# A decoder step's conv state leaves the chip in 44 narrow transposes instead of 5 wide ones

## The chip, the cores and the metric

The kernel runs on one core of a Trainium2 chip. The metric is the time of the device for one execution, in microseconds (us); lower is better. A core has TensorE (PE), VectorE (DVE), ScalarE (ACT), GpSimd (POOL) and SyncE (SP, which only issues transfers here). Each takes its instructions in order.

## The reference, cut to what matters

One inference step of a two-layer decoder (an S5 layer, then an attention layer called FoX), for a prompt of 512 tokens and 8 decode samples of one token. Each layer ends in a feed-forward block with a causal convolution of width 3:

```python
def causal_dwconv(u, prev, w, b):
    ext = jnp.concatenate([prev.astype(u.dtype), u], axis=1)
    y = ext[:, 0:t] * w[0] + ext[:, 1:1 + t] * w[1] + ext[:, 2:2 + t] * w[2]   # written as a loop
    return y + b, ext[:, t:]              # the last two rows are the new state

def conv_ffn(h, w_up, cw, cb, w_down, prev):
    u = h @ w_up                          # 1024 -> 5632
    y, new_prev = causal_dwconv(u, prev, cw, cb)
    g, val = jnp.split(y, 2, axis=-1)
    return (jax.nn.silu(g) * val) @ w_down, new_prev      # 2816 -> 1024
```

The state that is returned has two rows of 5632 floats for the prompt, and two for each of the 8 samples. The older sample row is a copy of an input. So ten rows of `u` come from the chip in each layer: the last two of the prompt and one of each sample.

## The kernel before, in words

Activations lie with the model dimension on the 128 partitions and the 520 tokens (512 + 8) along the free axis. A product goes panel by panel: a panel is 128 output columns of a weight matrix. SP loads its raw weights into one of two buffers (`weights`, L654), ACT rounds them to a high part (`w_hi`, L2311), POOL subtracts to get a low part (`w_lo`, L1001), and PE multiplies high by high, high by low and low by high for each block of 128 inputs, in two halves of the tokens (264 and 256 columns; `product`, L2872). Two slots of weights and two pairs of PSUM banks (`big`) alternate, so that PE works on one panel while the next is prepared.

The feed-forward block of layer `l` runs `up{l}0` (22 panels), `down{l}0` (8 panels over the first half of the 2816 inputs), `up{l}1` (22) and `down{l}1` (8, over the second half). In the up phases DVE scales a panel into `uc`, ACT copies the ten columns of the state into `newconv` (L2722) and makes the first tap of the convolution, and DVE makes the rest. There are 44 column tiles of 128 in all, one after each up panel.

`down{l}1` is where the state leaves. PE multiplies panels 0 to 5 one by one, and panels 6 and 7 together (`last_pair`, L2954), because the norm behind them wants the first half of the tokens early. DVE adds each panel to `y` (L1948) and sums its squares (L1252), ACT squares it. After panel 0 PE transposes `newconv`, which is laid out as [128, 10 rows, 44 tiles], in 5 transposes of 88 columns each (two rows x 44 tiles) with the helper `turn` (L3069), into two banks of the ring `misc`. DVE copies the banks into `crows`, which is the pair `yc` under another name (L1958), and SP stores row by row: 10 transfers of 44 pieces of 512 bytes, issued after the weights of panel 4 of `down{l}1` (`conv_out`, L842).

The PSUM ring `misc` has four banks. Its jobs are numbered in one list (`misc_jobs`), PE takes a bank when the reader of the job four before has freed it, and the two sides count on the same list. The ring of `crows` buffers is freed by counting finished stores (`crows_out`). Behind `down01` SP issues a plain copy of the older sample rows from input to output (L641), and then the weights of the next phase, `win1` (L654). ACT rounds the first of these panels early, into a buffer of its own (`hi_first`, L2316), between its squares of panel 6 and of panel 7 (L2660).

Of the kernel before, what the change touches and what calls it, by code (L numbers as in the profile page):

```python
# [28 lines left out]
P = 128  # L29
# [82 lines left out]
def misc_jobs():  # L112

    jobs = [("lam",), ("rows",), ("xsT",)] + [("xT", k) for k in range(KD)] + [("ms", "x0", 0), ("ms", "x0", 1)]
    jobs += [("memT", a) for a in range(4)] + [("conv", l, a) for l in range(2) for a in range(2)]
    jobs += [("cT", 0), ("ms_mem",)] + [("state", l, a) for l in range(2) for a in range(2)]
    jobs += [("h0", ri, a) for ri in range(2) for a in range(2)]
    inputs = [[*[("bT", t, a) for a in range(TP // 2)], *[("V", t, a) for a in range((TP + 2) // 3)]]
              for t in range(THIRDS)]
    jobs += [("memtok", 0, m) for m in range(3)] + inputs[0] + [("memtok", 0, 3)] + [("memtok", 1, m) for m in range(4)]  # L120
    for t in range(THIRDS):
        jobs += inputs[t] if t else []
        jobs += [("Y", 0, a) for a in range(TG // 4) if t == 1]
        jobs += [("K", t, a) for a in range(TG // 4)] + [("qrow", 0, 1)] * (t == 0) + [("cT", t + 1)] * (t + 1 < THIRDS)
        jobs += [("Y", 1, a) for a in range(TG // 4) if t == 1]
    for a in range(0, TG // 4, 2):
        jobs += [("mq", 0, a + b) for b in range(2)] + [("Y", THIRDS - 1, a + e) for e in range(2)]
    jobs += [("mq", 0, b) for b in (4, 5)] + [("OT", 0, p) for p in LAST[0]] + [("fin", ri) for ri in range(2)]
    jobs += [("mq", 0, b) for b in (6, 7)]
    for l in range(2):  # L130
        if l == 0:
            jobs += [("mmaxT", l), ("mmax", l), ("mden", l), ("mpv", l), ("mfin", l)]
        else:
            jobs += [("qrow", l, a) for a in range(2)] + [("q", b, a) for b in range(2) for a in range(2)]
            jobs += [("qrow", l, 2)]
            for m in range(12):
                jobs += [("kvtok", m), ("kvsamp", m)]
                jobs += [("logf",)] * (m == LOGF_AT) + [("dtot",), ("dc", 0)] * (m == DECAY_AT) + [("dc", 1)] * (m == DECAY_AT + 1)
                jobs += [("q", b, a) for b in Q_PANEL if Q_PANEL[b] == m for a in range(2)]
            jobs += [("mpv", l), ("fpv", PV_BESIDE), ("mfin", l), ("fpv", PV_BESIDE + 1)]  # L140
        jobs += [("ms", f"o{l}", 0), ("ms", f"o{l}", 1), ("ms", f"f{l}", 0), ("ms", f"f{l}", 1)]
        jobs += [("cout", l, a) for a in range(2)]
        jobs += [("ms", f"d{l}", 0), ("ms", f"d{l}", 1)]
        if l == 0:
            jobs += [("ms", "x1", 0), ("ms", "x1", 1)]
    jobs += [("yT", c, a) for c, a in TURNED_OUT]
    return {name: j for j, name in enumerate(jobs)}
# [22 lines left out]
    return enumerate((n, k) for n in range(2) for k in range(KD))  # L170


CONV_ROWS = 2 * 2 * KF
CONV_SETS = ((0, 4), (4, 5))


FOX_PAIRS = HEADS // 2
# [143 lines left out]
def program(nc, I, O):  # L321
# [4 lines left out]
    with ctx:  # L326

        def sb(name, shape, dt=F32):
            return ctx.enter_context(nc.sbuf_tensor(name, shape, dt))
# [10 lines left out]
        convw = sb("convw", [P, 2, 4 * 2 * KF])  # L340
        convs = sb("convs", [P, 2, 2 * NB, 2 * KF])
        newconv_at = nc.sbuf_base
        newconv = sb("newconv", [P, 2 + NB, 2 * KF])
        stats_at = nc.sbuf_base
        rstd = sb("rstd", [P, NT])
        sd = sb("sd", [P, NT])
# [287 lines left out]
        def _(sp):  # L634
# [197 lines left out]
            weights("glu", cols(I["w_glu"][0]), beside_glu, start=2)  # L832
            weights("wout0", cols(I["w_out"][0]))

            def conv_out(l):

                for a_, (first, end) in enumerate(CONV_SETS):
                    sp.wait_ge(s_("crows_ready"), 2 * l + a_ + 1)
                    for r in range(2 * first, 2 * end):
                        dst = O["prompt_ffn_conv"][l, 0, r] if r < 2 else O["sample_ffn_conv"][l, r - 2, 1]  # L840
                        at = (r % 2) * 2 * KF
                        sp.dma_start(dst.rearrange("(t p) -> t p", p=P),  # L842
                                     crows[a_][at:at + 2 * KF, (r // 2 - first) * P:(r // 2 - first + 1) * P]
                                     ).then_inc(s_("crows_out"), 16)

            def page_id(n):
                return sp.value_load(pages[0:1, bass.ds(n, 1)], min_val=0, max_val=I["cache_k"].shape[0] - 1)
# [13 lines left out]
            def ffn_weights(l):  # L861
                if l == 0:
                    sp.wait_ge(s_("stored"), 16 * stores[0])
                    sp.wait_ge(s_("pages_in"), 16)
                for f in range(2):
                    wu = I["w_up"][l].rearrange("(k p) n -> p k n", p=P)

                    def up(i, wu=wu, f=f):

                        it, half = i  # L870
                        return wu[:, :, bass.ds(it * P + (f * KH + half * KF) * P, P)]

                    kb, n, base, _ = PH[f"up{l}{f}"]
                    with sp.Fori(0, KH) as it:
                        for half in range(2):
                            slot = (base + half) % 2
                            sp.wait_ge(lo_made, it * 2 + (base + half - 1))
                            sp.dma_start(raw[slot][:, 0:KD, :], up((it, half))).then_inc(raw_loaded[slot], 16)
                        for n in range(4 if l == f == 0 else 0):
                            past_logf(it * 4 + n)  # L880
                    weights(f"down{l}{f}", cols(I["w_down"][l], (f * KH * P, (f + 1) * KH * P)),
                            (lambda i: conv_out(l) if i == 4 else None) if f else None if l else rest_logf)

                store(O["sample_ffn_conv"][l, :, 0, :], I["state_ffn_conv"][l, :, 1, :])

# [84 lines left out]
                store(dst[:, 512 * a_:512 * a_ + 512], ytok[c][0:(P if c < 4 else NB), 512 * a_:512 * a_ + 512])  # L970

            sp.wait_ge(s_("stored"), 16 * stores[0])
            sp.wait_ge(s_("crows_out"), 16 * 2 * (2 + NB))
            for s in range(2):
                sp.wait_ge(s_(f"ktok_out{s}"), 16 * 3)


        @block.gpsimd
        def _(pool):
# [171 lines left out]
            def head_zeros(i):  # L1151

                if i in (3, 4):
                    pool.wait_ge(lo_made, PH["win1"][2] + i + 1)
                if i == 3:
                    pool.wait_ge(s_("crows_out"), 16 * (2 + NB))
                    own.tell(pool.memset(kh[DH:P, :, :], 0.0), s_("heads_set"), 1)
                    own.sync()
                elif i == 4:
                    own.tell(pool.memset(qh[DH:P, :, :], 1.0), s_("heads_set"), 2)  # L1160
                    own.sync()
                elif i == 5:
                    own.tell(pool.memset(kvs[:], 0.0), s_("heads_set"), 3)
                elif i == 6:
                    diagonal()
# [67 lines left out]
        def _(dve):  # L1233
# [707 lines left out]
            def copy_out(ph, add=None, conv=None):  # L1941

                for m in range(6):
                    q = PH[ph][2] + m
                    dve.wait_ge(panel_done, q + 1)
                    for n_, (c0, c1) in enumerate(HALF):
# [3 lines left out]
                            tell(ins, panel_read, q + 1)  # L1950
                        else:
                            do(ins)
                    for a_, (first, end) in enumerate(CONV_SETS) if conv is not None and m == 0 else ():
                        full(dve, ("cout", conv, a_))
                        if conv:
                            dve.wait_ge(s_("crows_out"), 16 * (2 + NB))
                        c = slice(0, (end - first) * P)
                        freed(own, V.tensor_copy(crows[a_][0:CONV_ROWS, c], bank(("cout", conv, a_))[0:CONV_ROWS, c]),  # L1958
                              ("cout", conv, a_))
                        mark(s_("crows_ready"))  # L1960
                    sum_step(m)
# [333 lines left out]
        def _(act):  # L2295
# [417 lines left out]
            def ffn(l):  # L2713
                for f in range(2):
# [3 lines left out]
                    def work(it, half):  # L2718
                        fb = it + (f * KH + half * KF)
                        uu, yy = uc[half], yc[half]  # L2720
                        act.wait_ge(panel_read, it * 2 + (base + half + 1))
                        A.activation(newconv[:, :, bass.ds(fb, 1)].rearrange("p t a -> p (t a)"),  # L2722
                                     uu[:, T:T + 2 + NB], ACT.Copy).then_inc(act_step, 1)

                        act.wait_ge(s_("h_made"), it + (done + 1))
# [105 lines left out]
        def _(pe):  # L2831
# [615 lines left out]
            def ffn(l):  # L3447
                for f in range(2):
# [9 lines left out]
                    for m in range(n - 2):  # L3458
                        product(base + m, (base + m) % 2, kb, h_half, HALF, h_made if m == 0 else None)
                        if m == 0:  # L3460
                            pe.wait_ge(s_("tap_made"), 44 * (l + 1))
                            rows_ = newconv[:].rearrange("p r t -> p (r t)")
                            for a_, (first, end) in enumerate(CONV_SETS):
                                o = take(("cout", l, a_))
                                for n_ in range(first, end):
                                    ins = turn(o[0:CONV_ROWS, (n_ - first) * P:(n_ - first + 1) * P],
                                               rows_[:, CONV_ROWS * n_:CONV_ROWS * (n_ + 1)], P)
                                give(ins, ("cout", l, a_))
                    last_pair(f"down{l}1", h_half, f"d{l}")

            ffn(0)
# [238 lines left out]
```

## Time and profile before

| | us |
|---|---|
| median of 3 runs | 1484.91 |
| lowest, highest | 1484.53, 1489.85 |
| the profiled execution | 1484.91 |
| its span in the profile | 1483.2 |
| PE busy | 1395.6 |
| DVE, ACT, POOL busy | 958.5, 576.4, 638.0 |

The profiled execution is itself the median, and 1.7 us of it lie outside the span of the profile. PE is the engine with the most work; how far the others matter has to be read stage by stage.

### The profile page before, as it was taken

How to read it: one execution, taken by the hardware profiler on the slowest of the kernel's cores; microseconds unless marked ns; L12 is line 12 of the kernel's file. 1: busy time of each engine (PE TensorE's matmuls, PEld its weight loads, DVE VectorE, ACT ScalarE, POOL GpSimd, SP SyncE). 2: the span in 40 equal slices, each digit the busy share in tenths (PEclk: the TensorE clock that was granted, in tenths of full speed). 3: DMA queues.
4: the chain of work that ended last, by engine and by line, in shares of the span. 5: the costliest groups of instructions: out<-in, count | busy, mean ns of one | idle time of the engine just before them, and what ended most of it. 6: DMA issues, size and time to landing. Idle time of an engine off the chain costs nothing.

```text
span 1483.2 us, 33390 instructions
## 1 busy us (share of the span) xinstructions
PE 1395.6 (94%) x12587; PEld 1299.3 (88%) x12587; DVE 958.5 (65%) x1606; ACT 576.4 (39%) x1025; POOL 638.0 (43%) x416
## 2 busy tenths in 40 slices
PE   6988878989999999999899989999999999999998
PEld 6986667989999999999889956557889999999997
DVE  5779887577772177765657788653676761377755
ACT  4554355354432134323434235432454431243323
POOL 1589432303444334442369878302214343343441
PEclk9997889999999999999999999999999999999999
DMA  6363364313333233332337669995222333233331
GB/s 174 103 146 74 66 160 137 100 46 100 88 99 100 76 86 98 93 102 87 91 86 203 198 194 308 323 338 157 84 60 85 95 97 92 80 91 93 112 90 59
DMA packets 289761, 180.53 MB, mean 122 GB/s; under 512 B 54264, under 2 KB 275468, under 8 KB 289600
## 3 DMA queue, kind: packets, MB, share of 16 engines
q1 hardware_dynamic: 289088, 179.07, 41.8%
q8 instruction: 65, 1.06, 0.3%
q14 instruction: 32, 0.26, 0.1%
q10 hardware_dynamic: 576, 0.13, 0.0%
HBM read 167.10 MB, written 10.63 MB: 120 GB/s over the span
## 4 chain that ended last, share of the span: by engine, by line
PE 66%; DVE 11%; issue 9%; POOL 6%; ACT 3%; SPq 2%; DMA 2%; DVEq 0%; ACTq 0%; POOLq 0%
PE big L2872 54%; PE big L2954 3%; SPq L638 1%; PE misc L3069 1%; DVE y L1900 1%; POOL s5s L1005 1%; POOL e_tmp L1005 1%; DVE x L1909 1%; DVE x_lo L1327 1%; POOL w_lo L1001 1%; PE misc L2939 1%; PE misc L3209 1%; POOL e_r L1005 1%; DVE sc L2096 1%; PE big L2986 1%
## 5 line engine op out<-in xcount | busy, mean ns | idle before, releaser
L1001 POOL TENSOR_TENSOR w_lo<-raw,w_hi 128x1024 fp32r<-128x1024 f32 (+2 forms) x151 | 388.9, 2576 | 696.2 <-ACT w_hi L2311 467.3
L2311 ACT ACTIVATE w_hi<-raw 128x1024 fp32r<-128x1024 f32 (+2 forms) x172 | 191.3, 1113 | 552.1 <-PE big L2872 529.9
L2872 PE MATMUL big<-x_hi,w_hi 128*128 128x264 f32 (+1 forms) x1948 | 398.3, 286 | 5.5 <-DVE x_lo L1325 1.6
L2872 PE MATMUL big<-x_hi,w_lo 128*128 128x264 f32 (+1 forms) x1948 | 392.9, 283 | 0.0
L2872 PE MATMUL big<-x_lo,w_hi 128*128 128x264 f32 (+1 forms) x1948 | 391.1, 282 | 0.0
L2872 PEld LDWEIGHTS big<-x_hi,w_hi 128*128 128x128 f32 x1948 | 299.7, 188 | 9.8 <-issue 3.2
L2872 PEld LDWEIGHTS big<-x_lo,w_hi 128*128 128x128 f32 x1948 | 299.4, 188 | 0.0
L2872 PEld LDWEIGHTS big<-x_hi,w_lo 128*128 128x128 f32 x1948 | 299.3, 188 | 0.0
L1997 DVE SCALAR_TENSOR_TENSOR yc<-uc,convw,yc 128x512 f32<-128x512 f32 x88 | 137.2, 1559 | 112.6 <-ACT yc L2726 112.6
L2872 PE MATMUL big<-h_hi,w_hi 128*128 128x264 f32 x616 | 124.4, 283 | 6.3 <-DVE h_lo L2012 6.3
L2872 PE MATMUL big<-h_hi,w_lo 128*128 128x264 f32 x616 | 124.0, 282 | 0.0
L2872 PE MATMUL big<-h_lo,w_hi 128*128 128x264 f32 x616 | 123.9, 282 | 0.0
L2872 PEld LDWEIGHTS big<-h_hi,w_hi 128*128 128x128 f32 x616 | 94.1, 188 | 7.2 <-DVE h_lo L2012 7.2
L2872 PEld LDWEIGHTS big<-h_lo,w_hi 128*128 128x128 f32 x616 | 94.4, 188 | 0.0
L2872 PEld LDWEIGHTS big<-h_hi,w_lo 128*128 128x128 f32 x616 | 94.4, 188 | 0.0
L1136 POOL TENSOR_TENSOR areas<-areas,qb 128x768 f32<-128x768 f32 x41 | 75.0, 1838 | 10.3 <-DMA areas<-in_cache_k 9.3
L2025 DVE COPY y<-big 128x264 f32 (+1 forms) x32 | 12.2, 424 | 102.3 <-PE big L2872 102.3
L2002 DVE SCALAR_TENSOR_TENSOR yc<-uc,convw,yc 128x512 f32<-128x512 f32 x88 | 66.1, 752 | 12.7 <-DVE yc L2000 0.3
L2726 ACT ACTIVATE yc<-uc,convw 128x520 f32<-128x520 f32 x88 | 72.3, 821 | 0.8
L1252 DVE TENSOR_TENSOR sumsq<-sumsq,sq 128x520 f32<-128x520 f32 x20 | 57.7, 2885 | 20.5 <-ACT sq L2674 20.5
L2383 ACT ACTIVATE x_hi<-x,gains 128x264 fp32r<-128x264 f32 (+2 forms) x64 | 35.3, 561 | 36.9 <-DVE x L1909 29.0
L2722 ACT ACTIVATE newconv<-uc 128x10 f32 (+1 forms) x88 | 19.4, 221 | 69.2 <-DVE uc L1993 69.0
(491 smaller groups left out, 2326.0 us busy)
## 6 DMA issues: line engine op xcount, KB each, us to landing
raw<-in_w_up SPq DMA_DIRECT2D x88, 512.0 KB, 3.9
raw<-in_w_down SPq DMA_DIRECT2D x32, 704.0 KB, 4.7
areas<-in_cache_k SPq DMA_DIRECT2D x41, 384.0 KB, 4.3
areas<-in_cache_v SPq DMA_DIRECT2D x41, 384.0 KB, 4.5
raw<-in_w_in SPq DMA_DIRECT2D x16, 512.0 KB, 4.2
raw<-in_w_out SPq DMA_DIRECT2D x16, 512.0 KB, 4.2
raw<-in_w_kv SPq DMA_DIRECT2D x12, 512.0 KB, 4.0
spare<-in_cache_k SPq DMA_DIRECT2D x12, 384.0 KB, 4.6
```

The costliest lines, as they stand in the source:

```text
L1001: pool.tensor_tensor(w_lo[slot][:, 0:kb, :], raw[slot][:, 0:kb, :], w_hi[slot][:, 0:kb, :].bitcast(F32), ALU.subtract).then_inc(lo_made, 1)
L1005: own.do(pool.tensor_tensor(o, a_, b_, op))
L1136: own.tell(pool.tensor_tensor(p, p, qb[b % 2][:].rearrange("p (a d) -> p a d", a=2), ALU.mult), s_("k_product"), n + 1)
L1252: ins = V.tensor_tensor(sumsq[:], sumsq[:], sq[:, m % 2, :], ALU.add)
L1997: st(V.scalar_tensor_tensor(yy[:, 0:T], uu[:, 1:1 + T], w_[1], yy[:, 0:T], ALU.mult, ALU.add))
L2002: st(V.scalar_tensor_tensor(yy[:, 0:T], uu[:, 0:T], w_[0], yy[:, 0:T], ALU.mult, ALU.add))
L2311: A.activation(w_hi[slot][:, 0:kb, :], raw[slot][:, 0:kb, :], ACT.Copy).then_inc(hi_made, 1)
L2383: ins = A.activation(o, src, ACT.Copy, scale=1.0 if g is None else g)
L2722: A.activation(newconv[:, :, bass.ds(fb, 1)].rearrange("p t a -> p (t a)"), uu[:, T:T + 2 + NB], ACT.Copy).then_inc(act_step, 1)
L2726: A.activation(yy[:], uu[:, 2:2 + NT], ACT.Identity, bias=convw[:, 1 - l, bass.ds(it + (f * KH + half * KF + 132), 1)], scale=convw[:, 1 - ...
L2872: ins = pe.matmul(big[2 * slot + b_][:, 0:c1 - c0], w[:, k, :], r[:, c0:c1], start=(k == 0 and n_ == 0), stop=(k == kb - 1 and n_ == 2))
L2954: return pe.matmul(big[2 * slot + b_][:, 0:c1 - c0], w[slot][:, k, :], r[:, c0:c1], start=(k == 0 and n_ == 0), stop=(k == kb - 1 and n_ = ...
```

## The change

`newconv` is laid out as [128, 44 tiles, 10 rows], so that the ten columns of a tile lie together. Each tile is transposed by itself: 128 x 10 to 10 x 128. Four tiles fill a bank, and such a bank holds 512 neighbouring floats of each of the ten rows. There are 11 banks in a layer. PE makes two of them after each of panels 0 to 4 and the last after panel 5, DVE copies each ([10, 512]) to one of the two `crows`, and SP stores each with two transfers (2 rows and 8 rows of 2048 bytes). SP issues those of panels 0 to 3 behind the weights of panels 4 to 7 and those of panels 4 and 5 after the loop, ahead of the copy of the older rows. DVE waits, before it overwrites a `crows` buffer, for the two stores from it.

```diff
-        jobs += [("cout", l, a) for a in range(2)]
+        jobs += [("cout", l, a) for a in range(KF * 2 // 4)]
...
-CONV_ROWS = 2 * 2 * KF
-CONV_SETS = ((0, 4), (4, 5))
+def conv_rows(m):
+
+    return range(2 * m, min(2 * m + 2, 2 * KF // 4))
...
-        newconv = sb("newconv", [P, 2 + NB, 2 * KF])
+        newconv = sb("newconv", [P, 2 * KF, 2 + NB])
...
-            def conv_out(l):
-
-                for a_, (first, end) in enumerate(CONV_SETS):
-                    sp.wait_ge(s_("crows_ready"), 2 * l + a_ + 1)
-                    for r in range(2 * first, 2 * end):
-                        dst = O["prompt_ffn_conv"][l, 0, r] if r < 2 else O["sample_ffn_conv"][l, r - 2, 1]
-                        at = (r % 2) * 2 * KF
-                        sp.dma_start(dst.rearrange("(t p) -> t p", p=P),
-                                     crows[a_][at:at + 2 * KF, (r // 2 - first) * P:(r // 2 - first + 1) * P]
-                                     ).then_inc(s_("crows_out"), 16)
+            def conv_out(l, m):
+
+                for a_ in conv_rows(m) if m >= 0 else ():
+                    sp.wait_ge(s_("crows_ready"), 11 * l + a_ + 1)
+                    c = slice(4 * P * a_, 4 * P * (a_ + 1))
+                    for dst, r in ((O["prompt_ffn_conv"][l, 0][:, c], slice(0, 2)),
+                                   (O["sample_ffn_conv"][l, :, 1, c], slice(2, 2 + NB))):
+                        sp.dma_start(dst, crows[a_ % 2][r, 0:4 * P]).then_inc(s_(f"crows_out{a_ % 2}"), 16)
...
-                            (lambda i: conv_out(l) if i == 4 else None) if f else None if l else rest_logf)
+                            (lambda i: conv_out(l, i - 4)) if f else None if l else rest_logf)
+                for m in range(4, 8):
+                    conv_out(l, m)
...
-            sp.wait_ge(s_("crows_out"), 16 * 2 * (2 + NB))
...
+                sp.wait_ge(s_(f"crows_out{s}"), 16 * 2 * (12 - 2 * s))
...
-                    pool.wait_ge(s_("crows_out"), 16 * (2 + NB))
+                    for s in range(2):
+                        pool.wait_ge(s_(f"crows_out{s}"), 32 * (6 - s))
...
-                    for a_, (first, end) in enumerate(CONV_SETS) if conv is not None and m == 0 else ():
+                    for a_ in conv_rows(m) if conv is not None else ():
                         full(dve, ("cout", conv, a_))
-                        if conv:
-                            dve.wait_ge(s_("crows_out"), 16 * (2 + NB))
-                        c = slice(0, (end - first) * P)
-                        freed(own, V.tensor_copy(crows[a_][0:CONV_ROWS, c], bank(("cout", conv, a_))[0:CONV_ROWS, c]),
+                        if 11 * conv + a_ >= 2:
+                            before = (a_ // 2 + (conv * (6 - a_ % 2)))
+                            dve.wait_ge(s_(f"crows_out{a_ % 2}"), 32 * before)
+                        freed(own, V.tensor_copy(crows[a_ % 2][0:2 + NB, 0:4 * P], bank(("cout", conv, a_))[0:2 + NB, :]),
...
-                        A.activation(newconv[:, :, bass.ds(fb, 1)].rearrange("p t a -> p (t a)"),
+                        A.activation(newconv[:, bass.ds(fb, 1), :].rearrange("p a t -> p (a t)"),
...
-                            rows_ = newconv[:].rearrange("p r t -> p (r t)")
-                            for a_, (first, end) in enumerate(CONV_SETS):
-                                o = take(("cout", l, a_))
-                                for n_ in range(first, end):
-                                    ins = turn(o[0:CONV_ROWS, (n_ - first) * P:(n_ - first + 1) * P],
-                                               rows_[:, CONV_ROWS * n_:CONV_ROWS * (n_ + 1)], P)
-                                give(ins, ("cout", l, a_))
+                        for a_ in conv_rows(m):
+                            o = take(("cout", l, a_))
+                            for n_ in range(4):
+                                ins = turn(o[0:2 + NB, n_ * P:n_ * P + P], newconv[:, 4 * a_ + n_, :], P)
+                            give(ins, ("cout", l, a_))
```

## Rows read from the trace of the kernel before

**Rows 1.** The page: busy time of each engine, and the chain by line.

```profile
PE 1395.6 (94%) x12587; PEld 1299.3 (88%) x12587; DVE 958.5 (65%) x1606; ACT 576.4 (39%) x1025; POOL 638.0 (43%) x416
...
PE big L2872 54%; PE big L2954 3%; SPq L638 1%; PE misc L3069 1%; DVE y L1900 1%; POOL s5s L1005 1%; POOL e_tmp L1005 1%; DVE x L1909 1%; DVE x_lo L1327 1%; POOL w_lo L1001 1%; PE misc L2939 1%; PE misc L3209 1%; POOL e_r L1005 1%; DVE sc L2096 1%; PE big L2986 1%
```

**Rows 2.** Windows: length, busy per engine (PE, PEld, DVE, ACT, POOL), clock, DMA share.

```profile
583.00:645.37 62.37, 60.79 (x507) 60.58 (x505) 45.85 (x82) 23.88 (x35) 25.77 (x10) 1.00 0.36 105
...
658.00:671.00 13.00, 13.00 (x111) 13.00 (x110) 6.46 (x5) 2.20 (x3) 4.76 (x2) 1.00 0.36 106
...
710.00:724.00 14.00, 12.57 (x148) 11.69 (x148) 10.46 (x28) 8.91 (x23) 0.00 (x0) 0.88 0.12 35
```

**Rows 3.** The chain in order of time, layer 0: start, length, what.

```profile
646.36 0.55 PE misc L3069 x5
646.90 39.61 PE big L2872 x330
```

**Rows 4.** The same chain in layer 1, panels 1 to 5.

```profile
1410.63 39.61 PE big L2872 x330
```

**Rows 5.** The instructions that touch newconv: ns min/median/max, first and last start.

```profile
L2722 ACT ACTIVATE newconv<-uc x88: 202/221/224, 328.6 to 1401.8; 128x10 f32 x76, 128x10 f32<-128x10 f32 x12
L3069 PEld LDWEIGHTS misc<-ident,newconv x10: 120/122/123, 646.1 to 1410.3; 128*88 128x88 f32 x10
L3069 PE MATMUL misc<-ident,newconv x10: 270/272/273, 646.2 to 1410.4; 128*88 128x128 f32 x10
```

**Rows 6.** Weight loads around these transposes, layer 0: start, length, what.

```profile
646.09 0.55 PEld L3069 LDWEIGHTS misc<-ident,newconv 128*88 128x88 f32 x5
646.63 0.30 PEld L2872 LDWEIGHTS big<-h_hi,w_hi 128*128 128x128 f32 x2
```

**Rows 7.** Weight loads of the last output transposes: 12, then starts near the end.

```profile
1478.49 1.24 PEld L3069 LDWEIGHTS misc<-ident,x 128*128 128x128 f32 x12 [1.28 <-DVE x L1909]
...
1479.32 0.31 PEld L3069 LDWEIGHTS misc<-ident,x 128*8 128x8 f32 x3
...
1479.43 0.31 PEld L3069 LDWEIGHTS misc<-ident,x 128*8 128x8 f32 x3
```

**Rows 8.** The same 12 weight loads as a group: ns min/median/max.

```profile
L3069 PEld LDWEIGHTS misc<-ident,x x12: 87/140/144, 1478.5 to 1479.6; 128*128 128x128 f32 x8, 128*8 128x8 f32 x4
```

**Rows 9.** DVE in order of time, panels 0 and 1 of the down phase.

```profile
647.07 0.68 DVE L1958 COPY yc<-misc 88x512 f32<-88x512 f32 x1
647.90 0.29 DVE L1958 COPY yc<-misc 88x128 f32<-88x128 f32 x1
...
654.87 0.76 DVE L1948 TENSOR_TENSOR y<-y,big 128x264 f32<-128x264 f32 x2 [3.50 <-PE big L2872]
656.81 3.30 DVE L1252 TENSOR_TENSOR sumsq<-sumsq,sq 128x520 f32<-128x520 f32 x1 [1.18 <-ACT sq L2674]
```

**Rows 10.** POOL in order of time, same stretch.

```profile
656.33 3.22 POOL L1001 TENSOR_TENSOR w_lo<-raw,w_hi 128x1408 fp32r<-128x1408 f32 x1 [5.25 <-ACT w_hi L2311]
```

**Rows 11.** SP's transfers in order of time, from panel 1 to the next phase.

```profile
651.10 0.37 SPq L654 DMA_DIRECT2D raw<-in_w_down  x1
...
652.56 3.10 SPq L842 DMA_DIRECT2D out_sample_ffn_conv<-yc  x8
...
675.83 0.82 SPq L641 DMA_DIRECT2D out_sample_ffn_conv<-in_state_ffn_conv  x1
...
683.33 0.38 SPq L654 DMA_DIRECT2D raw<-in_w_in  x1
```

**Rows 12.** That last transfer's issue: KB, us from issue to landing.

```profile
raw<-in_w_in SPq DMA_DIRECT2D x1, 512.0 KB, 4.3
```

**Rows 13.** ACT in order of time, behind panel 5.

```profile
692.56 1.04 ACT L2316 ACTIVATE first_hi<-raw 128x1024 fp32r<-128x1024 f32 x1
695.05 0.43 ACT L2660 ACTIVATE sq<-y 128x264 f32<-128x264 f32 x1 [1.45 <-DVE y L1935]
```

## The prediction

> **What bounds the kernel now.** I read the page first, for the engine with the most work: PE is busy 94% of the span, and its panel product alone is 54% of the chain that ended last [rows 1]. An average says nothing of one stage, so I cut the stretch around the change into windows. In the second half of layer 0's up phase PE is busy 60.79 of 62.37 us, and in the down phase behind it 13.00 of 13.00, at full clock (granted 1.00, the 2.4 GHz level), while DVE works 6.46 and POOL 4.76 of those 13 us [rows 2]. Then I followed the chain in order of time through that phase. The five transposes stand in it by themselves, for 0.55 us, and behind them 330 matmul records in a single piece of 39.61 us, which are the five panels 1 to 5: 7.92 us each, with nothing between them [rows 3]. Layer 1 repeats it to the hundredth [rows 4]. So in this phase anything that PE does besides is paid in full, and what DVE, ACT, POOL and SP do is free up to the slack that they have. The last look was at the spacing of the transposes: the page's duration of one (272 ns [rows 5]) is its latency in a pipeline, and not what it costs.
>
> **The change on PE.** It takes away 5 transposes a layer and puts in 44. What one costs is the distance between starts: the five wide ones start their weight loads at 646.09 and the next ordinary load starts at 646.63 [rows 6], which is 0.54 us for five, 0.108 us each, waits for two banks included. The chain says the same, 0.55. The new ones are narrower: their stationary operand has 10 columns in place of 88, while the moving operand stays the 128 columns of the identity. The nearest rows are transposes of 8 columns at the end of the kernel: two of their loads start at 1479.32 and 1479.43, 0.11 us apart, and the whole dozen (8 of 128 columns, 4 of 8) keeps one pace, 11 distances in about 1.24 - 0.087 = 1.15 us, 0.105 each [rows 7, 8]. So the width of the stationary side doesn't show in the pace. I take 0.108.
>
> - Added: 44 x 0.108 = 4.75 us a layer. Removed: 0.54. Net 4.21 a layer, 8.42 in both. With 0.105 and nothing else it is 2 x (4.62 - 0.54) = 8.16.
> - The groups are now six in a layer, not one (8, 8, 8, 8, 8 and 4 transposes). Five at 0.108 and twelve at 0.105 leave some 0.015 us of fixed cost for a group, under 0.2 us in both layers. I take nothing for it beside the 0.108.
>
> The Trainium skill says, on the page "TensorE: Matmul & The Clock Gate", section "LDWEIGHTS (loading the stationary operand)", that a weight load takes a time in proportion to its columns. By that the new transposes' loads would take almost nothing. The rows agree in direction only, since the shortest record falls from 120 ns at 88 columns to 87 at 8 and the starts stay 0.11 apart; what it would make of the sum is rival 1.
>
> **The change on the others, panels 0 to 4.** Everything below is relative to the end T of a panel; in the trace of before DVE and ACT start at T.
>
> - DVE copies two banks a panel in place of two in the phase. A copy of 512 columns took 0.68 us and one of 128 took 0.29 [rows 9]: it goes by columns, so [10, 512] is 0.68, and seven and a half us a layer in all. It reads the panel till T+0.76, copies till about T+2.4, and then sums squares. That sum is the cover: it starts at T+1.94 now and takes 3.30 us, and it ends only 0.56 us after POOL's `w_lo`, which holds T+1.46 to T+4.68 [rows 9, 10]. A sum that starts at T+2.4 or even T+4.6 would end at the same T+5.2, if what it waits for is POOL. If it really needs 3.3 us of its own it ends at T+5.7 and still has over 2 us before the next panel. Cost 0; with the cover gone at most 1.4 us a panel on DVE.
> - DVE also waits for the stores out of `crows`, and behind it wait its sum, the bank that it frees (needed by PE two panels later) and SP. SP issues the stores of panel 0 after the weights of panel 4, at 651.5, 3.4 us before panel 1 ends, with the weights ahead of them in the queue; they land at about T+1 to T+2 of panel 1. From panel 2 on the stores before are issued at T+5.1 of the panel before (where SP passes its weights) and land some 5 us later, about T+1.5 of the next, whose T is 0.86 us later than now. So it waits about a microsecond with the copy, inside the same cover. Cost 0.
> - PE needs the bank of the fourth job before: read two panels ago. Cost 0.
> - ACT writes ten neighbouring floats in place of ten 176 bytes apart. The records are 202 to 224 ns for a fixed small size [rows 5]. PE waits for this branch only at the ends of the four up phases, so even a fifth of it gone (0.04 x 4) is 0.2 us; a loss would be as small. I take 0.
> - SP issues 22 transfers a layer in place of 10, for the same bytes. Eight of those of now took 3.10 us, 0.39 each [rows 11], and it has 7.9 us a panel. Cost 0. POOL's wait ahead of `win1` is for stores long done. Cost 0.
>
> **The step that isn't free by construction: SP behind panel 5.** The last bank (panel 5) is now stored before SP goes on to the copy of the older rows and to the first weights of `win1`. T is 646.90 + 39.61 = 686.5. DVE reads till T+0.8, copies till T+1.4, SP hears of it at T+1.5, two stores take 0.8, the copy of the older rows 0.82 [rows 11]: the weights are issued at T+3.2. They were issued at 683.33, T-3.2 [rows 11]. They land 4.3 us after issue [rows 12], at T+7.5; the copy of 176 KB just ahead of them may add up to 0.9. ACT wants them at 692.56 = T+6.1 for `first_hi`, so it starts 1.4 to 2.3 us late, takes 1.04, and ends at T+8.6 to T+9.5. Behind it stands the square of panel 7, at 695.05 = T+8.55 [rows 13], which will come 0.43 us later anyway, for the 4 transposes ahead of the last pair: T+8.98. So the slack is 0.4 us in the good case and short by 0.5 in the bad one. This happens in layer 0 only, since nothing follows layer 1's. I take 0.1 and keep 0 to 0.5.
>
> **Sum.** 8.42 + 0.1 = 8.5 us on a profiled execution of 1484.91, which is the median of the runs: 1493.4 us, 0.57% more. About 0.5% (7.4 us) is what a measurement of this kernel tells from no change, so the forecast is slower, and not by much beyond that bound.
>
> **Rivals.**
>
> 1. Narrow transposes are cheaper, so the time ends within 0.5%. Place: the same 88 positions on PE. If the weight load set the pace, it would be at most the 87 ns record of the 8-column load [rows 8]: 2 x (44 x 0.087 - 0.54) = 6.6 us, 1491.5. It decides from a pace under (7.42 / 2 + 0.54) / 44 = 0.0966 us. For it: the load record does get shorter. Against it: two narrow loads in a row start 0.11 apart [rows 7]. 0.15.
> 2. The weights of `win1` come later than I think, and PE waits. If the stores or the copy hold the queue 2 us more, ACT's square, the norm's sum and all behind it slip by 2 to 3 us once: 8.4 + 2.5 gives 1495.8. For it: three steps in a row with a 0.4 us margin. Against it: the queue is idle at that time. 0.15.
> 3. The shift meets slack further on, or the small stores turn out to have cost something now, and the whole is within 0.5% or better. The one soft place that I see is the norm between phases, where the granted clock was 0.88 for 14 us [rows 2]: of that stretch 24% lay at the 1.2 GHz level. Were it all full speed, at most 3.4 / 2 = 1.7 us would come back in such a place, and the other way round as much may be lost. That turns 1493.4 into 1491.7. A gain beyond 0.5% would need 16 us from somewhere, and I see no such row. 0.08 for within 0.5%, 0.03 for faster.
>
> The forecast itself has 0.59. Its own width is 8.2 to 9.0 us, with run-to-run spread 1492.7 to 1494.2. The range goes from 1490.9, a little under rival 1, to 1496.6, a little over rival 2; it leaves out about 2 in 10. Chances: slower by over 0.5% is the forecast and rival 2, 0.74; within 0.5% is rivals 1 and most of 3, 0.23; faster 0.03.
>
> **What the profile after would show.** 88 transposes of 128 x 10, in groups of 8 with starts 0.108 us apart; panels 0 to 5 of the down phase at intervals of 8.78 us where they were 7.92; the DVE sum of squares ending at the same T+5.2; no PE wait between these panels. The weights of `win1` issued some 3 us behind panel 5 and `first_hi` 1.4 us or more late, with the square behind it on time or half a microsecond late. The start of the up phases to the end of the span otherwise the same lengths. The prediction is wrong if the narrow pace is under 0.097 us, if PE waits for a bank or for a panel of weights in this phase, or if the first pair of `win1` starts more than 1 us late beside the shift.

## The result, and the profile after

| us | before | after |
|---|---|---|
| median (runs) | 1487.53 (6) | 1495.88 (6) |
| lowest, highest | 1484.53, 1489.85 | 1493.57, 1497.41 |
| the profiled execution, its span | 1484.91, 1483.2 | 1497.24, 1495.5 |

The changed kernel is slower: ratio 1.0062, 95% interval 1.005 to 1.0075. The table's medians of six runs give 1.0056. In all, 24 executions of the changed kernel were timed with this result, the profiled one among them: their median is 1497.05 (1492.47 to 1498.93), which is 9.5 us over the six runs of before and closer to the ratio. The median of before is 2.6 us above the three-run median that the prediction started from. First the page after, PE's busy time and the chain by line, as in [rows 1]:

```profile
PE 1405.8 (94%) x12665; PEld 1307.9 (87%) x12665; DVE 957.8 (64%) x1624; ACT 576.8 (39%) x1025; POOL 636.8 (43%) x416
...
PE big L2874 55%; PE big L2956 3%; PE misc L3071 2%; SPq L639 2%; DVE y L1902 1%; DVE x L1911 1%; DVE x_lo L1329 1%; POOL w_lo L1002 1%; ACT yc L2728 1%; PE misc L2941 1%; ACT w_hi L2313 1%; PE misc L3211 1%; PE big L2988 1%; PE misc L3216 1%; DVE sc L2098 1%
```

There are 78 more matmuls, which are 2 x (44 - 5). The transposes' line (L3071, L3069 before) has gone from 1% of the chain to 2%; DVE, ACT and POOL do the same work as before to 1.2 us. Where it stands shows in the chain in order of time through `down01`, as in [rows 3]:

```profile
647.27 0.99 PE big L2874 x6
648.26 0.87 PE misc L3071 x8
649.13 7.92 PE big L2874 x66
657.05 0.87 PE misc L3071 x8
657.92 7.92 PE big L2874 x66
665.84 0.87 PE misc L3071 x8
666.71 7.90 PE big L2874 x66
674.61 0.87 PE misc L3071 x8
675.49 7.88 PE big L2874 x66
683.37 0.87 PE misc L3071 x8
684.24 7.90 PE big L2874 x66
692.14 0.44 PE misc L3071 x4
692.58 9.47 PE big L2956 x78
```

The single piece of 39.61 us is cut into five panels, with 0.87 us of transposes ahead of each and 0.44 ahead of the last pair. The last pair starts 44.32 us after the end of panel 0, where it was 40.15 us: 4.17 more. Layer 1 has the same pieces. The instructions on `newconv`, as in [rows 5]:

```profile
L2724 ACT ACTIVATE newconv<-uc x88: 191/212/216, 330.3 to 1410.3; 128x10 f32 x76, 128x10 f32<-128x10 f32 x12
L3071 PEld LDWEIGHTS misc<-ident,newconv x88: 84/88/88, 648.0 to 1462.4; 128*10 128x10 f32 x88
L3071 PE MATMUL misc<-ident,newconv x88: 270/272/273, 648.1 to 1462.5; 128*10 128x128 f32 x88
```

The weight load's record fell from 122 ns to 88, but eight of them span 0.85 us and an ordinary load follows 0.86 us behind their first, which is 0.108 each (weight loads in order of time, as in [rows 6]):

```profile
656.79 0.85 PEld L3071 LDWEIGHTS misc<-ident,newconv 128*10 128x10 f32 x8
657.65 0.30 PEld L2874 LDWEIGHTS big<-h_hi,w_hi 128*128 128x128 f32 x2
```

DVE in order of time behind panel 2, as in [rows 9]. The first copy waits 1.81 us for the stores out of its buffer (0.24 and 0.36 us behind the next two panels). The sum of squares, which starts at 670.23, takes 0.88 us instead of 3.30:

```profile
665.88 0.76 DVE L1950 TENSOR_TENSOR y<-y,big 128x264 f32<-128x264 f32 x2 [3.55 <-PE big L2874]
668.45 0.68 DVE L1960 COPY yc<-misc 10x512 f32<-10x512 f32 x1 [1.81 <-DMA out_sample_ffn_conv<-yc]
669.35 0.68 DVE L1960 COPY yc<-misc 10x512 f32<-10x512 f32 x1 [0.22 <-DVE yc L1960]
670.23 0.88 DVE L1254 TENSOR_TENSOR sumsq<-sumsq,sq 128x520 f32<-128x520 f32 x1 [0.21 <-DVE yc L1960]
674.65 0.76 DVE L1950 TENSOR_TENSOR y<-y,big 128x264 f32<-128x264 f32 x2 [3.53 <-PE big L2874]
```

And POOL in the same stretch, as in [rows 10]:

```profile
667.33 3.22 POOL L1002 TENSOR_TENSOR w_lo<-raw,w_hi 128x1408 fp32r<-128x1408 f32 x1 [5.57 <-ACT w_hi L2313]
```

POOL ends at 670.55 and the sum at 671.11, 0.56 us behind it, as before. Behind panels 1, 3 and 4 the sum takes 2.33 to 2.59 us, since it starts longer ahead of POOL's end, and ends 0.55 or 0.56 us after POOL too. So the 3.30 us of before were a wait for POOL for the most part. The Trainium skill describes this on the page "SBUF — State Buffer", section "Terms": DVE and GpSimd share a port pair that is locked for a whole instruction, and the loser blocks. The trace agrees: the end of the sum goes by POOL's end and not by its own start.

SP and ACT behind panel 5, whose end T is 692.14, as in [rows 11, 13]:

```profile
693.89 0.28 SPq L843 DMA_DIRECT2D out_sample_ffn_conv<-yc  x1
694.21 0.82 SPq L642 DMA_DIRECT2D out_sample_ffn_conv<-in_state_ffn_conv  x1
695.08 2.20 SPq L655 DMA_DIRECT2D raw<-in_w_in  x2
```

```profile
699.60 1.06 ACT L2318 ACTIVATE first_hi<-raw 128x1024 fp32r<-128x1024 f32 x1 [1.32 <-DMA raw<-in_w_in]
701.13 0.43 ACT L2662 ACTIVATE sq<-y 128x264 f32<-128x264 f32 x1 [0.47 <-DVE y L1937]
```

The weights are issued at T+2.9, `first_hi` waits 1.32 us for them and ends 0.47 us before the square can start. The square is at T+9.0 and waits for DVE's copy of PE's result, not for the weights. PE's first matmul of the norm is at T+9.91 where it was at T+9.46, later by no more than the 0.44 us of the last four transposes. So this step cost nothing.

### The profile page after: what moved, and what is told of

Its sections match the earlier page's. It is cut to its first block, busy times and chain, and to the rows that moved or that the text cites. A ratio compares the mean times of both kernels' runs of the same rounds, so it can differ in the third digit from the quotient of the medians.

```text
span 1495.5 us, 33624 instructions
## 1 busy us (share of the span) xinstructions
PE 1405.8 (94%) x12665; PEld 1307.9 (87%) x12665; DVE 957.8 (64%) x1624; ACT 576.8 (39%) x1025; POOL 636.8 (43%) x416
## 4 chain that ended last, share of the span: by engine, by line
PE 69%; DVE 12%; issue 9%; ACT 3%; SPq 2%; POOL 2%; DMA 2%; DVEq 0%; ACTq 0%; POOLq 0%
PE big L2874 55%; PE big L2956 3%; PE misc L3071 2%; SPq L639 2%; DVE y L1902 1%; DVE x L1911 1%; DVE x_lo L1329 1%; POOL w_lo L1002 1%; ACT yc L2728 1%; PE misc L2941 1%; ACT w_hi L2313 1%; PE misc L3211 1%; PE big L2988 1%; PE misc L3216 1%; DVE sc L2098 1%
## 5 line engine op out<-in xcount | busy, mean ns | idle before, releaser
L1254 DVE TENSOR_TENSOR sumsq<-sumsq,sq 128x520 f32<-128x520 f32 x20 | 48.8, 2442 | 11.7 <-ACT sq L2676 9.9
```

The costliest lines, as they stand in the source:

```text
L1254: ins = V.tensor_tensor(sumsq[:], sumsq[:], sq[:, m % 2, :], ALU.add)
```

## The experiments

Ratios are to the kernel before, with 95% intervals. In each stretch of the profile below, "h to pair" is the time from the start of DVE's last `h_lo` of layer 0 to the start of PE's last pair: 41.89 us in the kernel before, 46.06 in the changed one. Its ends in the chain, two lines of before and the first of after (whose pair is at 692.58, above):

```profile
644.62 0.71 DVE h_lo L2012
686.51 9.45 PE big L2954 x78
```

```profile
646.52 0.71 DVE h_lo L2014
```

**e1. PE's part alone.** The kernel before, with 39 narrow transposes more in each layer, at one place.

```diff
                                 o = take(("cout", l, a_))
+                                for d_ in range(39 if a_ == 0 else 0):
+                                    turn(o[0:10, 0:P], rows_[:, 10 * d_:10 * d_ + 10], P)
```

> The kernel before with 39 more transposes of 128 x 10 in each layer, all at one place, ahead of the five wide ones (their result is overwritten). Layout, DVE copies, stores and order of SP are those of before. If PE's own time is the whole cost of the change (theory A), this costs 2 x 39 x 0.108 = 8.4 us over before: ratio 1.0057, and the group of 44 stands in the chain with 4.75 us. If a part of the change's cost comes from DVE's copies, the stores or SP's order (theory B), this costs less, 6 us or under (ratio under 1.004).

Measured: 1.0053 (1.0037 to 1.0068). The chain has the group of 44 as one piece of 4.80 us, and then the five panels as before:

```profile
647.54 4.80 PE misc L3069 x44
652.34 39.61 PE big L2872 x330
```

h to pair is 46.15. PE's part alone gives the changed kernel's stretch to 0.1 us, and spreading the groups over six places neither costs nor saves more than that.

**e2 and e10. The rest of the change alone.** The changed kernel with one transpose for each bank instead of four; three quarters of the stored state are left out. It ran twice, because the first result lay above the expectation.

```diff
-                            for n_ in range(4):
+                            for n_ in range(1):
```

> The changed kernel with one transpose in place of four for each of the 11 banks; three quarters of the state that is stored are left out. DVE's 11 copies, the 22 stores and SP's order are those of the change. Theory A: 11 transposes in place of 5, 2 x 6 x 0.108 = 1.3 us over before, ratio 1.001. Theory B: DVE, the stores or SP's order cost several us, ratio 1.002 or more over before.

> The quarter of the transposes once more (three quarters of the stored state are left out), for its size: it came out at 1.0022 with an interval of 1.0012 to 1.0032 where 1.0009 was expected. If DVE's copies, the stores and SP's order cost something, it comes out at 1.002 again and a segment of the profile between DVE's last h and the norm is longer than in the kernel before by more than the 0.65 us of 6 transposes. If not, it comes nearer to 1.0009 and the segments differ only where the kernel before differs from itself.

Measured: 1.0022 (1.0012 to 1.0032), then 1.0002 (0.9993 to 1.0012). Their mean is 1.0012 for an expected 1.0009. h to pair is 42.55 in both, 0.66 over before: six transposes of 0.108. In this stretch DVE's 11 copies, the 22 stores and SP's order are free. The two intervals don't meet although the program is the same, so two ratios can differ by 2 us by chance.

**e3. The cost doubled.** `for n_ in (0, 0, 1, 1, 2, 2, 3, 3)` in the changed kernel.

> The changed kernel with each transpose made twice, 88 in a layer. Theory A: 2 x 44 x 0.108 = 9.5 us over the changed kernel, 17.9 us over before, ratio 1.0121. If something hid a part of the 44 (a wait that would have been there anyway), the second 44 cost more than the first: ratio above 1.013.

Measured: 1.0123 (1.0102 to 1.0143). The pieces are 1.75 us for 16, and h to pair is 50.83, 4.77 over the changed kernel. The second 44 cost what the first did, so nothing had hidden a part of those.

**e4 and e5. The transposes in PE's wait.** In both they stand ahead of the last block of panel 0, where PE waits for DVE's last `h_lo`: 16 of the 44 in e4, all five wide ones in the kernel before in e5.

```diff
+                        def h_made_last(k):
+                            if k == KH - 1:
+                                pe.wait_ge(s_("tap_made"), 44 * (l + 1))
+                                state_out(range(4))          # in e5 the five wide transposes stand here
+                            h_made(k)
+
...
-                        product(base + m, (base + m) % 2, kb, h_half, HALF, h_made if m == 0 else None)
+                        product(base + m, (base + m) % 2, kb, h_half, HALF, h_made_last if m == 0 else None)
+                        if m >= 2:                           # e4 only
+                            state_out(conv_rows(m))
```

> The changed kernel with the first 16 of the 44 transposes moved ahead of the last block of panel 0 of the down phase, where PE waits 1.6 to 1.8 us for DVE's last h. The other 28 follow panels 2 to 5. Theory A says that PE time is free where PE waits: 16 x 0.108 = 1.73 us a layer go into the wait, less what is longer than it, so 3.2 to 3.5 us less than the changed kernel, 5 us over before, ratio 1.0034. If the transposes held back the h that PE waits for (through DVE or ACT), nothing is gained: ratio 1.006.

> The kernel before with its five wide transposes moved ahead of the last block of panel 0, into PE's wait for the last h. Theory A (PE time is free where PE waits): 0.54 us a layer goes into a wait of 1.6 to 1.8, so 1.1 us less than before, ratio 0.9993, and in the profile panel 0's last block starts as long after DVE's last h as now, with panel 1 directly behind it. If moving them costs what it saves, ratio 1.000 and the piece of 0.55 us stands in the chain at another place.

Measured: e4 1.0039 (1.0027 to 1.0052), h to pair 44.24, which is 1.82 less than in the changed kernel. e5 0.9981 (0.9967 to 0.9996), h to pair 41.35, 0.54 less than before. PE in order of time in the kernel before and in e5, layer 0:

```profile
645.37 0.51 PE L2872 MATMUL big<-h_hi,w_hi 128*128 128x264 f32 x2 [1.58 <-DVE h_lo L2012]
```

```profile
643.91 0.71 PE L3069 MATMUL misc<-ident,newconv 128*88 128x128 f32 x5
645.65 0.51 PE L2872 MATMUL big<-h_hi,w_hi 128*128 128x264 f32 x2 [1.03 <-DVE h_lo L2012]
```

PE still waits for `h_lo`, but for 1.03 us instead of 1.58. The profile supports 1.1 us of gain in both layers together. The 2.8 us that the ratio gives lie above it; its interval (0.6 to 4.9 us) holds both.

**e6. The shift of the ring.** The kernel before with a third, narrow job in the ring of `misc` banks in each layer, so that all later jobs get the banks that they have in the changed kernel.

```diff
-        jobs += [("cout", l, a) for a in range(2)]
+        jobs += [("cout", l, a) for a in range(3)]
...
+                            give(turn(take(("cout", l, 2))[0:10, 0:P], rows_[:, 0:10], P), ("cout", l, 2))
```

> The kernel before with one more job in the ring of misc banks in each layer (one narrow transpose and a DVE copy of 128 columns of it that nobody reads). The change adds 9 jobs a layer, and 9 is 1 modulo the 4 banks, so all later jobs get the same banks as in the changed kernel. Theory A: 2 x 0.108 = 0.2 us, ratio 1.000. The rival: the quarter of the transposes cost 3.2 us where 1.3 was expected, and the shift of the banks is where the other 2 us are, in the FoX stage or the wait ahead of wout1; then ratio 1.0014 or more.

Measured: 0.9995 (0.9983 to 1.0008). The shift of the banks shows no cost.

**e7. What sets the pace.** The changed kernel, each transpose over 64 of the 128 partitions; half of the stored state is left out.

```diff
-                                ins = turn(o[0:2 + NB, n_ * P:n_ * P + P], newconv[:, 4 * a_ + n_, :], P)
+                                ins = turn(o[0:2 + NB, n_ * P:n_ * P + DH], newconv[0:DH, 4 * a_ + n_, :], DH)
```

> The changed kernel with each transpose cut to 64 of the 128 partitions: the moving identity has 64 columns in place of 128, the stationary side stays 10 columns, the count stays 44. Half of the state that is stored is left out. If the moving columns set the pace, it falls to 0.054 us, and 2 x 44 x 0.054 = 4.75 us less than the changed kernel: ratio 1.0030 over before. If it is a cost for each instruction or the load (record of 88 ns), the starts stay 0.09 to 0.11 us apart: ratio 1.005 to 1.006.

Measured: 1.0051 (1.0033 to 1.0069). The chain:

```profile
654.18 0.54 PE misc L3071 x8
654.72 8.08 PE big L2874 x66
662.80 0.54 PE misc L3071 x8
663.34 8.12 PE big L2874 x66
```

Neither expectation was met in full: the ratio is that of the second, but the pace is neither 0.054 us nor 0.09 to 0.11. The piece of eight falls from 0.87 us to 0.54, 0.068 each. But each panel behind it is 0.2 us longer (8.08 to 8.13 for 7.90), so a panel with its group takes 8.64 us where it took 8.77. That is why the ratio moved by only 1.6 us: h to pair is 45.28, 0.78 less in a layer. Why the ordinary products lose 0.2 us behind transposes over half of the partitions wasn't tried further. Both sizes were changed at once here (rows of the stationary side and columns of the moving one), so which of them sets the pace stays open. The load is not it:

```profile
L3071 PEld LDWEIGHTS misc<-ident,newconv x88: 81/84/86, 645.4 to 1453.6; 64*10 64x10 f32 x88
```

Its record is 84 ns for 88, nearly as in the changed kernel, while the starts lie 0.068 us apart, closer than the record is long.

**e8. SP's step behind panel 5, made late.** The changed kernel with three copies of 176 KB more ahead of the weights of `win1`, in layer 0.

```diff
+                for i in range(3 if l == 0 else 0):
+                    sp.dma_start(zf[45056 * i:45056 * i + 45056].rearrange("(b f) -> b f", b=NB),
+                                 I["state_ffn_conv"][l, :, 1, :]).then_inc(s_("z_out"), 16)
                 store(O["sample_ffn_conv"][l, :, 0, :], I["state_ffn_conv"][l, :, 1, :])
...
```

> The changed kernel with three further copies of 176 KB (into scratch memory that nobody reads) ahead of the first weights of win1 on SP's queue, in layer 0 only. The profile of the changed kernel has that weight issue 3.0 us behind panel 5, its landing at 7.4, first_hi ending 0.47 us ahead of the square of panel 7. Three copies add 2.6 us of issuing and up to 1.4 us of transfer. Theory: the slack of 0.47 is used up and the rest is paid once, 2.1 to 3.5 us over the changed kernel, ratio 1.0076 to 1.0086 over before, with PE waiting at the norm behind down01. If first_hi were hidden by more than I think, ratio 1.006.

Measured: 1.0102 (1.0081 to 1.0123), more than expected. In the chain in order of time SP, the load and `first_hi` now stand where PE stood:

```profile
694.09 0.65 SPq L642
694.75 0.05 issue
694.80 5.49 DMA raw<-in_w_in
700.31 1.06 ACT first_hi L2323
701.37 0.32 ACT sq L2667
```

Windows over the norm, first of e8, then the same stretch (from T+10) of the changed kernel; columns as in [rows 2]:

```profile
700.00:707.00 7.00, 5.18 (x50) 5.12 (x51) 2.73 (x5) 1.69 (x3) 0.00 (x0) 0.76 0.37 108
```

```profile
702.00:709.00 7.00, 7.00 (x80) 6.91 (x80) 5.13 (x14) 2.60 (x7) 0.00 (x0) 1.00 0.27 77
```

Against the end of panel 5 the issue of the weights is 2.0 us later than in the changed kernel (T+4.9), the start of `first_hi` 2.95 us (T+10.4), and PE's first matmul of the norm 2.0 us (T+11.9). So some 0.9 us of the delay was hidden and 2.0 us were waited for. After PE's wait of 2.0 us the granted clock, 1.00 in the changed kernel, is 0.76 here: part of the window is at the 1.2 GHz level. The same matmuls take longer, first in e8, then in the changed kernel:

```profile
702.37 2.04 PE big L2961 x10
```

```profile
702.53 1.39 PE big L2956 x10
```

Four such pieces of the norm take 9.61 us for 8.00. From the end of panel 5 to POOL's first memset of `win1` it is 49.8 us against 46.1, 3.6 more: 2.0 of wait and 1.6 of slower PE. The other 2 us of the ratio lie within its interval.

**e9. SP's step, made early.** The changed kernel with the copy of the older rows ahead of the last stores.

> The changed kernel with the copy of the older rows issued ahead of the last stores of the state (behind the weights of panel 7) in place of behind them, so the first weights of win1 are issued 0.8 us earlier. Theory: first_hi starts 0.8 us earlier and the square of panel 7 and all behind it stay where they are, for they wait for PE; ratio 1.0057 to 1.006 over before, as the changed kernel. The rival: SP's order is the 1 to 2 us by which both the changed kernel (1.0062 for 1.0057) and the quarter of the transposes (1.0022 for 1.0009) came out above PE's share; then 1.005.

Measured: 1.0059 (1.0042 to 1.0077). ACT:

```profile
697.90 1.06 ACT L2318 ACTIVATE first_hi<-raw 128x1024 fp32r<-128x1024 f32 x1 [0.34 <-DMA raw<-in_w_in]
700.42 0.43 ACT L2662 ACTIVATE sq<-y 128x264 f32<-128x264 f32 x1 [1.46 <-DVE y L1937]
```

`first_hi` starts 1.0 us earlier after panel 5, and the square at the same T+9.0. So the step is free as it is and nothing is won by an earlier one; with `first_hi` 2.95 us later (e8) PE waits. From which delay on it costs was not run between these.

**e11 to e18. The two kernels again.** The changed kernel against the one before once more (e12), and further profiles of both.

> The kernel before, unchanged, for a second profile. The first one was 1484.91, at the low end of its runs (median 1487.5 to 1487.9 since). I expect a time of 1485 to 1490, with every stretch from DVE's last h to the end of the norm the same to 0.1 us, and the difference in the first 330 us, in the FoX stage and at wout1.

> The changed kernel once more. If the difference is PE's 8.4 us alone the ratio is 1.0057; the first measurement was 1.0062 with an interval of 1.005 to 1.0075.

> The changed kernel, a third profile. If the fall of the clock at wout1 goes along with the change, the stretch from the first product of wout1 to the first newconv of layer 1 is 75.5 us here too; if it is chance, it is 74.0 or 75.5.

> The kernel before, a third profile. If the fall of the clock at wout1 goes along with the change, that stretch is 74.0 us, as in its two other profiles; if it is chance, 74.0 or 75.5.

> The changed kernel, a fourth profile: 75.5 us if the fall goes along with the change, 74.0 or 75.5 if it is chance.

> The kernel before, a fourth profile: 74.0 us if the fall goes along with the change, 74.0 or 75.5 if it is chance.

> The changed kernel, a fifth profile: 75.5 us from wout1's first product to layer 1's first newconv if the fall goes along with the change, 74.0 or 75.5 if it is chance.

> The kernel before, a fifth profile: 74.0 us if the fall goes along with the change, 74.0 or 75.5 if it is chance.

Measured: e12 1.0065 (1.0053 to 1.0077). With the first pair there are five profiles of each kernel, cut here at the starts of named instructions, the last pair's as in the chain (lowest to highest of five, us):

| stretch | before | after |
|---|---|---|
| start to layer 0's first `newconv` | 328.6 to 330.9 | 329.3 to 330.3 |
| from there to the last pair of `down01` | 357.9 to 358.2 | 362.0 to 362.3 |
| to the first FoX score | 176.6 | 176.6 to 176.7 |
| to the first product of `wout1` | 152.4 to 155.9 | 154.4 to 158.8 |
| to layer 1's first `newconv` | 74.0 to 75.6 | 74.0 to 76.0 |
| to its last `newconv` | 309.5 to 309.8 | 310.0 to 310.2 |
| to the end | 80.6 to 81.3 | 84.7 to 85.3 |
| span | 1482.3 to 1485.7 | 1492.0 to 1497.9 |

Three rows differ by more than their spread: the two that hold a down phase (4.16 and 4.07 us by their means) and the up phases of layer 1 (0.4). The rest varies within one kernel about as much as between the two, although its means lie 2.3 us apart in sum, 1.6 of them in the row of the FoX stage that ends at `wout1`. The step of 1.5 us at `wout1` is such a case. In windows of 8 us from its first product, the kernel before (first profile) and its fourth:

```profile
1018.00:1026.00 8.00, 7.93 (x65) 7.93 (x66) 0.91 (x3) 1.69 (x2) 3.09 (x3) 1.00 0.44 131
```

```profile
1016.25:1024.25 8.00, 8.00 (x56) 8.00 (x56) 0.68 (x3) 0.42 (x1) 1.35 (x1) 0.79 0.44 131
```

The clock fell in two of five profiles of before and in four of five of after, and e2 and e10, which are one program, have it once (75.55 us against 74.02). So it happens without the change; whether the change makes it likelier, these counts can't say. What PE did ahead of it doesn't tell the cases apart: in the 8 us before this product it was busy 8.00 us at a granted clock of 1.00 both in the fourth profile of before, where the clock fell, and in the third, where it didn't.

## Why the prediction was right and where its number was off

- **PE's sum.** 4.21 us a layer was forecast from a pace of 0.108; the stretches give 4.16 and 4.07. The pace is 0.108 (0.87 for eight), and e1, e2 and e3 scale with the count. Shown. The panels between the groups are 7.88 to 7.92 us where all were 7.92, which takes 0.1 us off.
- **Rival 1, narrow transposes are cheaper.** It did not happen. By the Trainium skill's page "TensorE: Matmul & The Clock Gate", section "LDWEIGHTS (loading the stationary operand)", the load's time goes by its columns; its record did fall from 122 to 88 ns, less than in proportion, and the starts stayed 0.108 us apart. In e7 they lay closer than the record is long, so the record does not set the pace.
- **DVE, the stores, PE's banks.** Forecast at 0, and no cost shows (h to pair in e2 and e10, the ratio of e6). DVE waited up to 1.8 us for stores, where about 1 was forecast, and its sum still ended at T+5.3, as worked out from POOL's end.
- **SP behind panel 5.** T+3.2 for the issue and T+7.5 for the landing were forecast; 2.9 and 7.5 came. I had 0.1 us for it and 0.4 of slack; it was 0 and 0.47. Rival 2 did not happen, and e8 shows its mechanism: SP held up by the 2 us that the rival names cost 3.6 us in the profile, where the rival had 2.5, since the slower clock adds 1.6 to the wait.
- **The layout of newconv.** ACT's write is about 10 ns shorter, and I took 0. The up phases of layer 1 are 0.4 us longer in each profile of the changed kernel and of its variants, and not in e1, e5 or e6, which have the old layout: PE waits 0.6 us for `w_lo` in their first panels and not 0.3, and 1.70 us for `h_lo` in the first down panel and not 1.58. That this comes from the layout, and not from another part of the changed program, was not tried.
- **The level.** The step that failed is the last of the sum, "8.5 us on a profiled execution of 1484.91, which is the median of the runs", with its width for the forecast, "with run-to-run spread 1492.7 to 1494.2". That execution was at the low end: six runs gave a median of 1487.53, the medians of 16 to 24 runs beside the experiments are 1487.57 to 1488.43, and single runs of the kernel before go from 1483.05 to 1492.58. The width left some 0.4 us for the spread, though the three runs at hand already lay 5.3 us apart. The forecast of 1493.4 lies 2.5 us under the six-run median (1495.88) and 3.6 under the median of all 24 executions (1497.05), and 2.6 of that is the base. The range ended at 1496.6: it holds the first of these medians and not the second, nor the profiled execution (1497.24).
- **The size of the change.** 8.5 us (1.0057) lies in the interval of the measured ratio (1.005 to 1.0075) and is near what the stable stretches sum to (4.16 + 4.07 + 0.42 = 8.65). That it is so near is in part luck: PE's share came out 0.2 us under the 8.42, SP's 0.1 did not come, and the 0.4 us of the up phases, taken at 0, made up for both.

What stays open is a remainder of half to two and a half us: the two ratios of the changed kernel give 9.2 and 9.7 us, the mean spans of the five profiles 11.0, the stable stretches 8.65. It lies in the FoX stage and at `wout1`, whose spread in one kernel is as large (3.5 and 1.5 us), so that no run shows whether it belongs to the change.

## What to carry to other kernels

On the engine that sets the end, price a small operation by the distance between starts of its nearest relatives, times the count, and not by how little data it has: ten columns cost what 88 did. Work of that engine is free only in a place where it waits; moving the five transposes of before by one block into such a wait gave the only gain over the kernel before, 0.54 us a layer. And take the base from many runs, with their spread: a change of half a per cent (7.4 us) is no larger than the spread of one kernel's runs (1483.05 to 1492.58).

## What the runs showed that I had not expected

- A wait of PE of 2.0 us for a late transfer cost 3.6 us on the chain, as the granted clock was 0.76 and not 1.00 over the 7 us around and behind it (e8).
- Transposes over 64 partitions start 0.068 us apart, and the panel behind each group is 0.2 us longer (e7).
- The same program's first panel of `wout1` runs at a granted clock of 1.00 or 0.79 without any difference in the program, 1.5 us apart, and its FoX stage varies by 3.5 us (e11 to e18).
